# Delta-rule mixer: both directions held at once, 16-row diagonal blocks inverted row by row in packed form, decays exponentiated straight out of PSUM

## The reference, cut to what matters

```python
def gated_delta_chunked(q, k, v, beta, log_decay, s0):      # chunks of c tokens
    gam = jnp.cumsum(log_decay, axis=-1)
    decay = where(incl, exp(gam[i] - gam[j]), 0)             # lower triangle
    kk = einsum('bhnid,bhnjd->bhnij', k, k)
    t_mat = eye(c) + where(strict, kk * decay, 0) * beta[i]
    u  = solve(t_mat, v * beta)                              # unit lower triangular
    wk = solve(t_mat, k * (beta * exp(gam)))
    k_dec = k * exp(gam[-1] - gam);  chunk_decay = exp(gam[-1])
    def step(s, ...):                                        # serial over chunks
        w = u_c - wk_c @ s
        o = (q * exp(gam)) @ s + (q k^T * decay) @ w
        return chunk_decay * s + k_dec^T @ w, o

even_mixer: oc_f, sc_f = gated(context, forward);  oc_b, sc_b = gated(context, flipped)
            ol_f = gated(latent, forward, sc_f);   ol_b = gated(latent, flipped, sc_b)
            y = even_output(ol_f + flip(ol_b), ...)
each layer: modulation = silu(c) @ ada_w + ada_b  (6 * 1024 columns), norm, mixer, expert-choice FFN
```

## Time and profile before

| what | value |
|---|---|
| median of 3 runs | 1546.08 us (1544.28 to 1550.96) |
| the profiled execution: its time / span of the core | 1542.72 us / 1540.8 us |
| PE busy | 1298.3 us, 84% |
| DVE, ACT, POOL busy | 612.0, 410.9, 114.2 us |
| mean granted TensorE clock | 0.931 |

### The profile page before, as it was taken

The page is one execution under the profiler, slowest core; times in us unless marked ns, Lnnn a source line. Parts: engine busy times, 40 slices in busy tenths (PEclk is TensorE's granted clock), DMA queues, the critical chain, the costliest instruction groups (busy, mean ns, idle before and its releaser), DMA issues.

```text
span 1540.8 us, 20716 instructions
## 1 busy us (share of the span) xinstructions
PE 1298.3 (84%) x8879; PEld 968.0 (63%) x8879; DVE 612.0 (40%) x1109; ACT 410.9 (27%) x723; POOL 114.2 (7%) x160
## 2 busy tenths in 40 slices
PE   6999899899889765567999965556899999999987
PEld 3648788778768312124899621122599968999856
DVE  1433744364445100002665400001398456455574
ACT  2323222132123000001433200000254556243462
POOL 4000133233400000000000000000000000000000
PEclk9999899999989988889999987888999989999988
DMA  8713354364327799999453799999734411444100
GB/s 283 272 55 128 122 188 164 110 219 164 110 66 283 305 409 409 409 409 402 175 199 137 312 410 409 409 409 409 290 110 165 164 56 57 168 158 164 56 1 28
DMA packets 125103, 338.73 MB, mean 220 GB/s; under 512 B 8657, under 2 KB 11590, under 8 KB 125014
## 3 DMA queue, kind: packets, MB, share of 16 engines
q1 hardware_dynamic: 117536, 334.51, 57.3%
q10 hardware_dynamic: 7478, 2.91, 0.8%
HBM read 336.35 MB, written 1.05 MB: 219 GB/s over the span
## 4 chain that ended last, share of the span: by engine, by line
PE 64%; DMA 16%; SPq 8%; DVE 7%; ACT 2%; issue 1%; POOL 0%; ACTq 0%; DVEq 0%
PE bank L582 8%; PE bank L584 8%; PE bank L583 8%; DMA weight_ring<-in_w_up_dram 6%; PE bank L566 6%; SPq L1134 6%; PE bank L678 3%; DMA weight_ring<-in_w_gate_dram 3%; DMA weight_ring<-in_w_down_dram 3%; DMA expert_slots<-in_w_down_dram 3%; PE bank L508 3%; PE bank L692 3%; PE bank L854 3%; PE bank L697 2%; DVE arena L1698 2%; SPq L1139 2%
## 5 line engine op out<-in xcount | busy, mean ns | idle before, releaser
L582 PE MATMUL bank<-input_high,weights_high 128*128 128x256 f32 (+1 forms) x992 | 290.7, 293 | 6.6 <-DVE input_low L1698 6.6
L583 PE MATMUL bank<-input_low,weights_high 128*128 128x256 f32 (+1 forms) x992 | 284.0, 286 | 0.0
L584 PE MATMUL bank<-input_high,weights_low 128*128 128x256 f32 (+1 forms) x992 | 283.7, 286 | 0.0
L1698 DVE TENSOR_TENSOR arena<-arena,bank 128x512 f32<-128x512 f32 (+1 forms) x117 | 78.1, 667 | 360.1 <-PE bank L854 246.7
L1698 DVE TENSOR_TENSOR weights_low<-weight_ring,weights_high 128x1024 fp32r<-128x1024 f32 x124 | 151.7, 1224 | 145.2 <-ACT weights_high L1298 145.0
L582 PEld LDWEIGHTS bank<-input_high,weights_high 128*128 128x128 f32 x992 | 188.3, 190 | 11.6 <-issue 8.7
L584 PEld LDWEIGHTS bank<-input_high,weights_low 128*128 128x128 f32 x992 | 188.6, 190 | 0.0
L583 PEld LDWEIGHTS bank<-input_low,weights_high 128*128 128x128 f32 x992 | 188.1, 190 | 0.8
L1298 ACT ACTIVATE weights_high<-weight_ring 128x1024 fp32r<-128x1024 f32 x124 | 131.1, 1058 | 153.5 <-PE bank L584 142.8
L854 PE MATMUL bank<-weight_ring,arena 128*32 128x512 f32 x512 | 75.1, 721 | 57.3 <-DMA weight_ring<-in_w_up_dram 40.2
L566 PE MATMUL bank<-arena,weight_ring 128*128 128x256 f32 (+1 forms) x320 | 96.7, 464 | 0.0
(11 more groups left out here) (345 smaller groups left out, 1707.7 us busy)
## 6 DMA issues: line engine op xcount, KB each, us to landing
weight_ring<-in_ada_w_dram SPq DMA_DIRECT2D x24, 2048.0 KB, 7.9
weight_ring<-in_w_gate_dram SPq DMA_DIRECT2D x16, 2048.0 KB, 16.2
weight_ring<-in_w_down_dram SPq DMA_DIRECT2D x16, 2048.0 KB, 21.4
weight_ring<-in_w_up_dram SPq DMA_DIRECT2D x16, 2048.0 KB, 24.4
weight_ring<-in_even_w_in_dram SPq DMA_DIRECT2D x9, 2048.0 KB, 8.7
arena<-in_w_up_dram SPq DMA_DIRECT2D x8, 2048.0 KB, 20.8
expert_slots<-in_w_up_dram SPq DMA_DIRECT2D x8, 2048.0 KB, 23.9
arena<-in_w_gate_dram SPq DMA_DIRECT2D x8, 2048.0 KB, 23.7
```

The source lines that it names most:

```text
L582: pe.matmul(b[:, 0:width], hi[:, k, :], XHI[:, k, t0:t0 + width], start=k == 0, stop=False)
L583: pe.matmul(b[:, 0:width], hi[:, k, :], XLO[:, k, t0:t0 + width], start=False, stop=False)
L584: mm = pe.matmul(b[:, 0:width], lo[:, k, :], XHI[:, k, t0:t0 + width], start=False, stop=k == KD - 1)
L1698: return dve.tensor_tensor(out_, a, b, op)
```

## The change

Both directions share one list of steps, `mixer_steps()`. The second direction has tiles of its own (`backward_direction`, in the region that the split weights use later), so its steps can lie between those of the first.

- Decays. The cumulative log decays are turned into rows once (`ROWS`, high and low part). For a head PE selects its row with a one-column pattern (L726, L729, L730, fp32r) and adds a large number at the masked places with a bf16 product (L727, L731). ACT takes the exponentials directly from PSUM, with the column's value (and the log of beta, `GLB`) as bias. The subtraction, the two clips, the mask multiplication and the multiplication by beta on DVE are gone.
- Inverse. The levels 0 to 3 are gone. POOL masks A to its diagonal 16x16 blocks, DVE packs these by a sum into `PACK` (`pack`), the start is set (`seed`), and 14 links (`chain`, 28 for both directions) fill in one row each: one PE product against `ROW_OF`, a multiplication and a subtraction on DVE. Then DVE spreads the packed inverse to full tiles and PE turns them (`spread`). The levels 4, 5 and 6 stay as `turn` and `grow`; in place of the second product a PE transpose and an ACT copy make the other form (`flip`), for two of the three levels.
- `ada`: the turn against `SEL` is now four transposes, and DVE sums the parts. The decayed keys (`kdec`) are made by DVE, no longer by POOL.
- The first direction's `solve` and `walk` lie between the second's levels. The 20 `ada` steps are spread anew, five of them between the steps of the second walk.

```diff
-LEVELS = 7
+BASE = 16
+LEVELS = (4, 5, 6)
+    steps = ada + [("turnrows", 0, 0, 0), ("rows", 0, 0, 0)]
+    for i in range(2 * HEADS):
+        d, h = divmod(i, HEADS)
+        if i + 1 < 2 * HEADS:
+            steps += [("rows", (i + 1) // HEADS, (i + 1) % HEADS, 0)]
+        steps += link(0) if d else []
+        steps += [("kk", d, h, 0)]
+        steps += link(0) if d else []
+        steps += [("qk", d, h, 0)]
+        steps += link(0) if d else []
+        if h >= 1:
+            steps += [("pack", d, h - 1, 0)]
+        if h == HEADS - 1:
+            steps += [("pack", d, h, 0), ("seed", d, 0, 0)]
+        if i in (1, 3):
+            steps += ada
+        if i in (5, 6, 7):
+            steps += ada + link(0)
+    steps += link(0, BASE)
     for h in range(HEADS):
+        steps += [("spread", 0, h, 0)] + (link(1) if h % 2 else [])
+    for lv in LEVELS:
+        for slot in range(HEADS + 2):
+            steps += level(0, lv, slot) + (link(1) if slot < HEADS else [])
+            if slot == 2:
+                steps += ada
+    steps += link(1, BASE)
     for h in range(HEADS):
+        steps += [("spread", 1, h, 0)]
+    pieces = walk(0)
+    for lv in LEVELS:
+        for slot in range(HEADS + 2):
+            steps += level(1, lv, slot)
+            if lv == LEVELS[0] and slot < HEADS:
+                steps += [("solve", 0, slot, 0), ("kdec", 0, slot, 0)]
+            if lv == LEVELS[1] and slot >= 2 or lv == LEVELS[2] and slot < 3:
+                steps += pieces.pop(0)
...
+    for h in range(HEADS):
+        steps += [("solve", 1, h, 0), ("kdec", 1, h, 0)] + (ada if h % 2 else [])
+    for i, piece in enumerate(walk(1)):
+        steps += piece + (ada if i < 5 else [])
     return steps
...
-                for f in range(4):
-                    mm = pe.matmul(b[:, 2 * f:2 * f + 2], PART[:, f * P:f * P + P], SEL[:, :], start=True, stop=True)
+                mm = transposes(b, [(b[:, f * P:f * P + P], PART[:, f * P:f * P + P]) for f in range(4)])
...
+                elif kind == "chain":
+                    r, c0, c1 = base_row(d, a)
+                    pe.wait_ge(chain_ready[d], a)
+                    b = v_open()
+                    mm = pe.matmul(b[:, 0:16 * (c1 - c0)], ROW_OF[:, r, :], BASE_X[:, d, :, c0:c1], start=True, stop=True)
+                    v_close(mm, step)
...
+                elif kind == "flip":
+                    pe.wait_ge(*inverse_at[d, h])
+                    b = s_open()
+                    for u in range(UNITS):
+                        mm = pe.transpose(b[:, u * P:u * P + P], XnT[d][:, h, u, :], ident[:, :])
+                    plain_at[d, h] = (scalar_drained, s_close(mm, step))
...
+                elif kind == "rows":
+                    i = HEADS * d + h
+                    Tlo, Thi, Tq = decay_bufs[i % 2]
+                    if i >= 2:
+                        act.wait_ge(tri_ready, i - 1)
+                    b = take()
+                    for u in range(UNITS):
+                        ins = act.activation(Tlo[:, u, :], b[:, u * P:u * P + P], ACT.Exp, scale=-1.0, bias=GLB[:, u, i:i + 1])
+                    drained(ins)
+                    b = take()
+                    for u in range(TT):
+                        act.activation(Thi[:, u, :], b[:, u * P:u * P + P], ACT.Exp, bias=NGC[:, u, i:i + 1])
+                    drained(act.activation(Tq, bank(b[:, T:2 * T], 2, P), ACT.Exp))
...
+                elif kind == "pack":
+                    m = mask_of[step]
+                    dve.wait_ge(masked, m + 1)
+                    blocks = Amask[:, m % 2].rearrange("p u (k c) -> p u c k", c=BASE)
+                    dve.reduce_sum(PACK[:, d, 4 * h:4 * h + 4, :], blocks, AX.X).then_inc(packed, 1)
+                elif kind == "chain":
+                    r, c0, c1 = base_row(d, a)
+                    w = c1 - c0
+                    x_, t_ = BASE_X[:, d, :, c0:c1], STEP[:, 0:16 * w].rearrange("p (a b) -> p a b", a=16)
+                    b = take()
+                    drained(tt(t_, last(PACK[:, d, :, r], w), bank(b, 16, w), MUL), True)
+                    tt(x_, x_, t_, SUB).then_inc(chain_ready[d], 1)
```

568 lines of the change are left out of this document (307 added, 261 removed).

## The result

The changed kernel took 1467.16 us (median of 4 runs, 1466.72 to 1471.61), the kernel before, run beside it, 1548.52 us (4 runs, 1544.28 to 1555.02). The ratio is 0.948, its 95% interval 0.944 to 0.952: 81 us less. The forecast was 1449 us and 97 less, with a range of 1434 to 1470.

The account below looks back on a forecast made before the run. PE was taken to bound the mixer's levels, the walk its own chain. PE work 155.5, open waits 15 and half clock 6 made 176.5 us against 272, 95.5 less: 1449 us, range 1434 to 1470.

Parts of the forecast that it names:

- forecast's own case: Whole kernel: the predicted saving arrives and the time is 1438 to 1462 us, chance 0.64.
- forecast's own signs of being wrong: Mixer: links over 1.5 us, pack over 1, level waits for DVE, clock under 0.9, or L508 awaiting its load.
- PE's work, 75.3 us less: Mixer: PE's work at full clock falls from 230.8 to 155.5 us.
- rival 4: Mixer's PE transposes run at half rate, 20 us more, 1469 us; chance 0.04.
- Walks covered: Both walks: other PE work fills the waits between dependent products, all but the last output's.
- Setup 40 us: Stage ahead of the levels: 17 us for direction 0's heads, 23 for direction 1's, 6 us of it open.
- the half clock: New setup: PE often waits and runs partly at 1.2 GHz, 6 us added as an estimate.
- the links: Chain in direction 1's heads: a link takes about 1.1 us, 14 links 16 us.
- the spread: Ahead of the levels: DVE writes four tiles before PE's turns; 3 us open for direction 0, 2.5 for direction 1.
- Cost nothing: Weight loads issued later: they still arrive in time; only cover is lost, two loads of 5.4 us.
- Rival 3: Decayed keys and spreads: DVE and POOL block each other, at most 15 us, some 8 on the path, 1457; chance 0.05.
- Rival 2: Chain: 28 links at 2 us instead of 1.1 set the pace, 25 us more, 1474 us; chance 0.14.

Follow-up runs that it names:

- The blocks of 8: Changed kernel with 8x8 instead of 16x16 diagonal blocks: 6 links a direction instead of 14, one more level each; 1478.8 us.
- The kernel with the directions apart: Changed kernel with only the step order altered: direction 0's solve and walk end before direction 1's levels begin; 1483.3 us.
- kernel with three edits: Changed kernel plus small loads started early, unread PE products in its waits, and row selections over 128 rows instead of 48; 1454.3 us.
- the unused products: Changed kernel plus PE products that nothing reads, at four places where PE would wait; 1460.4 us.
- A move of the seed: Small loads early, unread PE products, 128-row selections, and direction 1's seed put behind direction 0's spreads, its links into the first level's slots; 1450.1 us.

## Why the prediction was right, and where it was off

The result lies in the range, at its slow end and by a narrow margin. It is outside the forecast's own case (1438 to 1462), in the part of the range that was there for rivals, and the unaltered kernel gave 1470.2 us the second time, with the range ending at 1470. The mechanism was right in what carries the gain: PE's work in the mixer and the waits of the old walks go. But nearly every size that was off was too small, and two of the forecast's own signs of being wrong came true, a pack over 1 us (1.02) and links over 1.5 us in part. Of the steps:

- **PE's work, 75.3 us less, and the pace in the levels.** Right: PE's busy time in the mixer fell from 250.8 us to 178.1, by 72.7. There are 192 records of each of the turns and the grows, and a flip's four transposes take 0.44 us (256.31 to 256.75 in PE's timeline). That speaks against rival 4, as does a clock of 1.00 from 240 us on, in levels with 16 flips and four of the spreads. The blocks of 8 show that PE's work counts nearly in full there.
- **Walks covered.** Right: no wait over 1 us, 0.85 at the last output. The kernel with the directions apart puts a price on it, 7 to 10 us.
- **"Setup 40 us" was the step that was too small.** Counted from 169 us, direction 0's last product k^T q ended after 25.8 us (17 taken), direction 1's heads 28.8 later (23), the first level product came 8.4 behind these (5), and 130.6 us to the end followed (125.5). These are 17.1 us over with the 6 for half clock counted once. In the kernel with three edits the same stretches are 16.8, 28.5 and 7.5 us: the clock and the selections explain direction 0's heads in full and direction 1's hardly at all. What was mis-sized:
  - the half clock: 8 to 9 us, 6 taken (the unused products took 8.7 off);
  - the selections: 1.39 us a head, 0.84 taken from the earlier trace rows. The nearest row by type was not the nearest by rows: the operand has 48, the row there 128;
  - the pack: 1.02, 0.69 taken, by the estimate above 1.3 us in all;
  - the links: about 1.1 us taken, 1.16 to 1.98 measured from start to start where no ada step stands between (1.50 and 1.59 at 217.59, 219.09, 220.68), 1.68 on average with the ada steps. PE and DVE wait for each other in turn there, with k k^T, k^T q and the pack in DVE's queue. Even with the full clock and the faster selections direction 1's heads took 28.5 us (185.8 to 214.3), 23 were forecast;
  - the spread: only its own four instructions were counted, not the packs and the seed of the other direction that stand ahead of them in DVE's queue. A move of the seed gave 2 us.
- **"Cost nothing" for the late loads failed.** The expert stage waited no longer, as forecast. But the four 2 MB loads now lie over the end of the mixer and beyond it, and the small loads that ACT starts there cost some 4 us: the first `up` load came 41.9 us behind the last output, 37.7 with these loads early. The forecast asked whether the large loads come in time, not what starts beside them.
- **Rival 3** happened, in part elsewhere than it said: in two decayed keys (1.38 us for 0.68, at 278.92 and 282.49), in no spread, and in direction 1's links (0.97 to 1.16 in place of 0.2 to 0.4), where it cost nothing in the chain. In the seed it cost up to 0.8 us ahead of the first spread. The Trainium skill (SBUF — State Buffer, Who interferes with whom) says that a VectorE instruction with two SBUF inputs contends with a GpSimd one that reads SBUF, and one with at most one such input, outside the two-port modes, does not. The kernel with the link through PSUM agrees, 0.40 us or less in every link. Rival 2 was partly true in direction 1's heads and nowhere else, and its 1474 us did not come; the measured time lies between the forecast's case and this one.

Between the two profiled executions the span fell by 75.8 us where 95.5 were forecast. Of the 20 us, 12 are the setup and the spreads, net of the 6 taken, 5 the levels and walks (a half clock until 234 us among them), 4.8 the stretch from the last output to the first `up` load (41.9 against 37.1 before), and the rest of the program gave 2 back. With the three edits and the seed moved, the mixer is 179.5 us, against the 176.5 forecast. Its levels and walks still take 4 us more than forecast (219.9 to 349.3, 125.5 taken). These are not waits: PE is busy 126.1 of these 129.4 us at a clock of 1.00, where the forecast had 119.5 of work and 6 open. So PE's work there was counted 6 us too small; which products are the dearer ones was not tried and stays open.

## What to carry to other kernels

When a stage is shortened, list every transfer that starts near its old and its new end, the small ones on other queues as well, and ask which now run beside large ones. For a product that the trace doesn't show, choose the near row by the shape of both operands, and read its price from the start of the next one, since its own duration can hide it. When work is interleaved, walk each in-order queue once at every joint: what stood behind the chain's instruction on VectorE, the other direction's packs and seed, set the start of the levels.

## What the runs showed of the hardware

- A group of five products, three of them with fp32r operands, took 1.39 us when these had 48 rows and 0.85 with 128 rows, 80 of them zeros.
- Of three small loads started in a row on ACT's queue beside 2 MB loads, the third start took 5.42 to 5.61 us in eight executions; two in a row beside such loads took 1.02 to 2.20 together, and three in a row without them 0.39 to 0.60 each. The 256 KB load landed 10.2 to 10.7 us after its start beside the large loads, 3.3 in the kernel before.
- The granted clock fell to 0.50 for several us behind places where PE had waited (3.46 us ahead of L702, 3.61 ahead of the first spread), and the stretch shifted by several us between two executions of the same kernel. Unused products in these waits kept it at 1.00 from 170 us to the end of the mixer.
- A sum of 128x512 to 128x64 on DVE took 1.02 us, where elementwise instructions of 512 columns took 0.69.
- In direction 1's heads a DVE instruction with two SBUF inputs and 16 to 240 columns took 0.97 to 1.16 us while a POOL mask over 512 columns ran, and 0.19 to 0.39 without one. With one of its inputs in PSUM a link's subtraction took 0.40 or less beside POOL too.
